# One stage for row norm, turn, product and head norms in five places of a two-block network, and expert prologues tile by tile

## The chip, the cores and the metric

The kernel runs on one core of a Trainium2 chip. The metric is the device time of one execution in microseconds. Five places and two expert layers are edited, so times of places are given from the start of the profiled span.

## The reference, cut to what matters

Two blocks are computed one after the other on 512 tokens of width 1024, all in float32. The first block has two layers, which also carry or read 256 context tokens; each is a mixer followed by an expert layer (16 experts, each with its own choice of tokens):

```
h = rms_norm(x, norm1_g[i]) * (1 + sc1) + sh1        # even: u = h @ ev_w_in; odd: u = h @ od_w_in
q, k = rms_norm(q, q_g), rms_norm(k, k_g)            # odd: 8 heads of 64, in the neighbourhood attention
x = x + g1 * y
h = rms_norm(x, norm2_g[i]) * (1 + sc2) + sh2
aff = softmax(h @ router); gate, idx = top_k(aff per expert); x = x + g2 * experts(h[idx])
```

The second block is a forgetting attention, a gated convolution FFN, a sparse attention on shared keys and values, and a second FFN:

```
proj = rms_norm(x, a_norm) @ a_w_in                  # 3 x 1024 columns for q, k, v and 16 forget columns
q, k = rms_norm(q, q_gain), rms_norm(k, k_gain)      # 16 heads of 64
log_f = log_sigmoid(proj[..., 3072:] + b_f); c = cumsum(log_f)
parts = rms_norm(x, kv_norm) @ kv_w                  # six parts of 2 x 64; ks, kw normed and rotated
proj = rms_norm(x, b_norm) @ b_w_in                  # 1024 columns for q (normed, rotated), 48 for gates
```

## The kernel before

Everything is a sequence of stages (class Stage, line 29): each is a block with one instruction list per engine, which end together before the next begins. Rows of x lie as tiles of 128 tokens (P = 128): LT = 4 tiles of x, CT = 2 of the context, NT = 6 in all. Each product is made of three matmuls, since float32 operands are split in a high part (written by ACT as fp32r) and a low part (the difference, written by DVE): hi x hi, hi x lo, lo x hi.

`norm_turn` (298) is a stage of its own: ACT squares all tiles (337), takes one root for all (340), DVE norms them (363), PE turns them with 512 columns a unit (406), ACT writes the high part with the gain (348, 350), DVE the low part (377); where there is a shift, POOL adds it to the low part (394). `linear` (412) is the next stage: SP asks for weight pieces of 256 columns (452), ACT makes their high part (505), DVE the low part (523), PE multiplies per tile ("tok": rows stationary, 256 weight columns moving) or per 128 weight columns ("feat": weights stationary, tokens moving) in line 493, and DVE keeps each result (540). It has RING = 3 weight slots and eight PSUM buffers. `linear_split` (548) is the like with pieces of 512 columns and half the rows of the weight (588, 602, 612). `head_norm` (634) is a third stage: squares on ACT (681), sums, root and multiply on DVE (697 to 705), the gain on POOL (671), then, with rope, the rotation on DVE (718 to 727).

The five places, in the order of time: (1) even_layer, 1543 and 1552, six tiles, with a shift; (2) odd_layer, 2362 to 2371, six tiles with a shift, whose Q, K and V each have 512 columns, with two stores beside the weights on POOL's queue (461), and two head norms; (3) forgetting, 2545 to 2564, four tiles, with two head norms after `forget_sums` (2458) and a small stage of constants; (4) sparse_attention, 2996 to 3014, the shared keys and values, with three head norms, of which the third is for the compressed keys (they need `compress`, 3010); (5) sparse_attention, 3021 to 3026, with one head norm with rope. In place 3 the forget gate F is a "tok" job of 16 columns, which `forget_sums` then turns on PE (2478).

`mixture` (1130) is one stage of an expert layer. SP loads the norm's gain and two (or one) rows of modulation, broadcast to all partitions (1224 to 1227), then router and four weight quarters. DVE combines the gains (1450) after ACT has squared all tiles (1382) and taken one root (1384), norms tile after tile (1460, 1462), PE turns each (1277), and after the last one PE multiplies all tiles with the router (1284). The softmax, the choice of tokens (1475 to 1477), the gathering by POOL and the stream of 192 weight quarters follow. `add_gated` (1624) is the output product in front of it, by `linear`.

The order on each engine is written out by hand in these functions, and semaphores alone join the engines.

## Time and profile before

| | us |
|---|---|
| median of 3 runs | 5204.43 (5191.65 to 5210.83) |
| the profiled execution, its own time | 5182.43 |
| its span in the trace | 5180.6 |
| PE busy | 4192.4 |
| DVE busy | 3071.3 |
| mean granted clock of PE | 0.879 of full speed |

The span is the time from the first to the last instruction in the trace; around it lie some 1.8 us. Busy is the time in which an engine had an instruction under way. A granted clock of 1 is 2.4 GHz, of 0.5 it is 1.2 GHz. The kernel runs on one core, so no other core shares its time.

### The profile page before, as it was taken

The page shows a single profiled execution, that of the slowest core. Times are in us where ns is not written, and L with a number is a line of the kernel's source. Part 1 is how long each engine was busy: PE and PEld are TensorE (multiplying, and loading weights), DVE is VectorE, ACT ScalarE, POOL GpSimd, SP SyncE. Part 2 cuts the span into 40 slices and gives each one's busy share as a digit, 9 for nine tenths or more (in the row PEclk, how much of TensorE's full clock was granted, in tenths as well). Part 3 has the DMA queues.
Part 4 walks back from the last instruction along what each step waited for, and adds up shares of the span by engine and source line. Part 5 has one row for each costly group of instructions (what it writes and reads, how often), then busy time and mean ns, then how long its engine had stood idle before and what let it go on. Part 6 is the DMA issues. An engine that isn't in the chain of part 4 may idle for free. (4 is left out here: it accounts for less than half of the span.)

```text
span 5180.6 us, 68690 instructions
## 1 busy us (share of the span) xinstructions
PE 4192.4 (81%) x28028; PEld 3310.1 (64%) x28028; DVE 3071.3 (59%) x4349; ACT 1888.9 (36%) x2461; POOL 549.9 (11%) x419
## 2 busy tenths in 40 slices
PE   6868867999956887979669999686799856785998
PEld 2755665666656866869545555465687655674777
DVE  5259946888824556665458888436476234454672
ACT  4122324666622313222126666315322112352221
POOL 0111000111112003323001112002000001000000
PEclk9988787999978997978779999888899967897999
DMA  6120036999930220000249999400122201000322
GB/s 235 54 83 25 1 108 226 364 363 362 334 117 29 74 84 6 3 6 2 100 161 356 365 362 357 159 25 1 56 95 94 92 29 34 1 1 33 114 94 77
DMA packets 246407, 658.34 MB, mean 127 GB/s; under 512 B 27028, under 2 KB 91796, under 8 KB 245576
## 3 DMA queue, kind: packets, MB, share of 16 engines
q1 hardware_dynamic: 227808, 615.14, 33.3%
q0 software_dynamic: 8064, 30.46, 2.2%
q10 hardware_dynamic: 10224, 8.36, 0.5%
q8 instruction: 224, 3.67, 0.3%
q14 instruction: 87, 0.71, 0.0%
HBM read 624.97 MB, written 28.41 MB: 126 GB/s over the span
## 5 line engine op out<-in xcount | busy, mean ns | idle before, releaser
L1426 DVE TENSOR_TENSOR w_lo<-w_quarter,w_hi 128x2048 fp32r<-128x2048 f32 x384 | 874.0, 2287 | 200.0 <-ACT w_hi L1364 198.7
L1364 ACT ACTIVATE w_hi<-w_quarter 128x2048 fp32r<-128x2048 f32 x384 | 735.4, 1917 | 379.2 <-DMA w_quarter<-in_moe_w 188.3
L2682 DVE TENSOR_TENSOR w_lo<-w_chunks,w_hi 128x1024 fp32r<-128x1024 f32 x132 | 161.8, 1226 | 301.4 <-ACT w_hi L2660 301.4
L2634 PE MATMUL ffn_ps<-ffn_inT_hi,w_hi 128*128 128x512 f32 x704 | 276.4, 393 | 16.5 <-DVE w_lo L2682 16.5
L2634 PE MATMUL ffn_ps<-ffn_inT_lo,w_hi 128*128 128x512 f32 x704 | 275.9, 392 | 0.0
L2634 PE MATMUL ffn_ps<-ffn_inT_hi,w_lo 128*128 128x512 f32 x704 | 275.6, 391 | 0.0
L1265 POOL DMA_INDIRECT summed_dram<-gains_then_rows,row_token x32 | 137.9, 4310 | 1005.6 <-DVE gains_then_rows L1445 1005.6
L1312 PE MATMUL down_ps<-w_hi,hiddenT 128*96 128x512 f32 (+1 forms) x512 | 208.1, 406 | 39.2 <-DVE w_lo L1426 26.6
L900 PE MATMUL probT_ps<-ident,prob 128*128 128x128 f32 x896 | 164.6, 301 | 82.6 <-ACT prob L980 80.4
L967 ACT ACTIVATE probT<-probT_ps 128x256 f32<-128x256 f32 (+4 forms) x272 | 142.2, 523 | 223.5 <-PE probT_ps L900 223.5
L1312 PE MATMUL gate_ps<-w_hi,rowsT 128*96 128x512 f32 (+1 forms) x512 | 206.2, 403 | 12.5 <-DVE w_lo L1426 9.6
L1312 PE MATMUL up_ps<-w_hi,rowsT 128*96 128x512 f32 (+1 forms) x512 | 204.7, 400 | 7.4 <-DVE w_lo L1426 7.4
L2660 ACT ACTIVATE w_hi<-w_chunks 128x1024 fp32r<-128x1024 f32 x132 | 138.5, 1049 | 189.4 <-PE ffn_ps L2647 163.7
L1314 PE MATMUL gate_ps<-w_lo,rowsT 128*96 128x512 f32 (+1 forms) x512 | 204.4, 399 | 0.0
L1314 PE MATMUL down_ps<-w_lo,hiddenT 128*96 128x512 f32 (+1 forms) x512 | 204.2, 399 | 0.0
L1314 PE MATMUL up_ps<-w_lo,rowsT 128*96 128x512 f32 (+1 forms) x512 | 201.8, 394 | 0.0
L980 ACT ACTIVATE prob<-score_ps,negmax 128x256 f32<-128x256 f32 (+4 forms) x272 | 166.1, 611 | 87.2 <-DVE negmax L949 85.2
L588 PE MATMUL lin_ps<-w_hi,haT 128*128 128x512 f32 (+1 forms) x576 | 178.8, 391 | 23.3 <-DVE w_lo L612 23.3
L406 PE MATMUL turn_ps<-ident,normed 128*128 128x128 f32 x286 | 58.1, 377 | 166.1 <-DVE normed L363 153.5
L505 ACT ACTIVATE w_hi<-w_landing 128x2048 fp32r<-128x2048 f32 (+4 forms) x39 | 64.7, 1661 | 343.5 <-PE lin_ps L493 221.8
L900 PEld LDWEIGHTS probT_ps<-ident,prob 128*128 128x128 f32 x896 | 106.4, 150 | 126.2 <-ACT prob L980 118.3
L612 DVE TENSOR_TENSOR w_lo<-w_landing,w_hi 128x2048 fp32r<-128x2048 f32 (+2 forms) x28 | 56.2, 2007 | 184.4 <-ACT w_hi L602 184.4
(648 smaller groups left out, 10173.8 us busy)
## 6 DMA issues: line engine op xcount, KB each, us to landing
w_quarter<-in_moe_w SPq DMA_DIRECT2D x384, 1024.0 KB, 6.5
w_chunks<-in_f_w_up SPq DMA_DIRECT2D x88, 512.0 KB, 3.2
ada_landing<-in_ada_w SPq DMA_DIRECT2D x24, 1024.0 KB, 7.0
ada_ring<-in_ada_w SPq DMA_DIRECT2D x24, 1024.0 KB, 5.2
w_chunks<-in_f_w_down SPq DMA_DIRECT2D x44, 512.0 KB, 3.2
w_landing<-in_od_w_in SPq DMA_DIRECT2D x13, 1024.0 KB, 7.2
w_landing<-in_a_w_in SPq DMA_DIRECT2D x12, 1024.0 KB, 5.1
w_landing<-in_ev_w_in SPq DMA_DIRECT2D x6, 1024.0 KB, 7.4
```

The costliest lines, as they stand in the source:

```text
L588: mm = nc.tensor.matmul(ps[n % 2][i][:, 0:width], h[:, g * HK + k, cols], v[:, c % NP, k, 0:width], start=(g + k + j == 0), stop=(g == 1 a ...
L900: mm = nc.tensor.transpose(tps(a, b), pr[:, i % SB, a:b], ident)
L967: nc.scalar.activation(pT[:, i % SB, 0:n], tps(0, n), ACT.Copy).then_inc(tkept, 1)
L980: nc.scalar.activation(pr[:, i % SB, 0:u[1]], score(i, 0, u[1]), ACT.Exp, bias=mx[:, m:m + 1], scale=scale, accum_out=sm[:, m:m + 1]).then ...
L1265: nc.gpsimd.indirect_dma_start(out=sum_dram, out_offset=bass.IndirectOffsetOnAxis(ap=idx[:, e:e + 1], axis=0), in_=ys[e % 2], in_offset=No ...
L1312: nc.tensor.matmul(out[0:R, cols], v[0][:, k, :], wh[c][:, kk, cols], start=first, stop=False, skip_group_check=True)
L1314: nc.tensor.matmul(out[0:R, cols], v[0][:, k, :], wl[c][:, kk, cols], start=False, stop=False, skip_group_check=True)
L1364: nc.scalar.activation(wh[g % NP][:, :, :], land[g % NL][:, :, :], ACT.Copy).then_inc(hi_ready, 1)
L1426: tt(wl[g % NP][:, :, :], land[g % NL][:, :, :], wh[g % NP][:, :, :].bitcast(F32), ALU.subtract) \
L2634: mm = nc.tensor.matmul(ps[c % 4][:, :], w[:, c % NP, cols], h[:, k, :], start=(k + i == 0), stop=(k == KD - 1 and i == 2))
L2660: nc.scalar.activation(wh[:, c % NP, :], land[:, c % NL, :], ACT.Copy).then_inc(hi_ready, 1)
L2682: nc.vector.tensor_tensor(wl[:, c % NP, :], land[:, c % NL, :], wh[:, c % NP, :].bitcast(F32), ALU.subtract).then_inc(split, 1)
```

## The change

`normed_linear` is new and takes the place of norm_turn, linear (or linear_split) and head_norm in the five places. Weight pieces are asked for from the stage's start. Roots, norms, turns, high and low parts go tile by tile, and PE multiplies a tile with the first piece as soon as it is split; turning uses 128 columns an instruction where 512 were used. The shift is added by DVE together with the gain, no longer by POOL. It has four PSUM buffers for products and four for turns, and pieces of 256 columns. Heads are normed by chunks of four heads (a piece), two and three pieces behind the product: squares and root on ACT, sum, multiply and rope on DVE, gain on POOL. In place 2 K comes first, then Q and V; in place 4 the tok job comes before the feat job; the third head norm of place 4 stays a stage. Places 1 and 4 have RING = 2, the others 3. The forget columns become a feat job: 16 weight columns stationary, 512 tokens moving, so F is already turned in forget_sums.

In both expert layers the broadcast gains are loaded by POOL's queue beside the output product in front (`RowGains`), and DVE combines them there after its second piece; roots are taken tile by tile, and the router's product of a tile follows the turn of the next. The odd layer's output product has three weight slots where it had two.

The diff, cut to its core:

```diff
@@ linear @@
-def linear(nc, h, K, w, jobs, RING=3, whole=None, low_from=None, beside=(), mod=None):
+def linear(nc, h, K, w, jobs, RING=3, whole=None, low_from=None, beside=(), mod=None, then=None):
...
+                if c == 1 and then is not None:
+                    dve.wait_ge(beside_done, 16 * len(beside))
+                    then()
@@ new function @@
+def normed_linear(nc, x, segments, h, w, jobs, ident, heads=(), RING=3, beside=()):
...
+    PW, NB, HK, HD = 256, 4, KD // 2, 64
+    wv = w.rearrange("(k p) n -> p k n", p=P)
+    pieces = [(job, a, min(a + PW, job[2])) for job in jobs for a in range(0, job[2], PW)]
...
+            for c, (job, a, b) in enumerate(pieces):
+                if c >= RING:
+                    sp.wait_ge(split, c - RING + 1)
+                sp.dma_start(land[:, c % RING, :, 0:b - a], wv[:, :, job[1] + a:job[1] + b]).then_inc(landed[c % RING], 16)
+
+        @block.gpsimd
+        def _(pool):
+            if beside:
+                pool.wait_ge(rows_split, 2 * nt)
+            for dst, src in beside:
+                pool.dma_start(dst, src).then_inc(beside_done, 16)
+            for i, c in enumerate(order):
+                z, gain, _, _ = normed_heads[c]
+                pool.wait_ge(head_normed, i + 1)
+                nc.gpsimd.tensor_tensor(z, z, gain.unsqueeze(1).unsqueeze(1).broadcast_to(list(z.shape)), ALU.mult) \
+                    .then_inc(head_gained, 1)
+            if order:
+                pool.wait_ge(head_gained, len(order))
+            if beside:
+                pool.wait_ge(beside_done, 16 * len(beside))
+
+        @block.tensor
+        def _(pe):
+            def turn_tile(i):
+                pe.wait_ge(normed, i + 1)
+                for half in range(2):
+                    if i >= 2:
+                        pe.wait_ge(rows_split if not shifted else moved, 2 * (i - 2) + half + 1)
+                    for k in range(HK):
+                        kk = half * HK + k
+                        mm = nc.tensor.transpose(tp[i % 2 * 2 + half][:, k, :], xn[:, i % 2, kk * P:(kk + 1) * P],
+                                                 ident)
+                    mm.then_inc(turned, 1)
+
+            u = 0
+            turn_tile(0)
+            turn_tile(1)
+            for c, piece in enumerate(pieces):
+                job, a, b = piece
+                pe.wait_ge(split, c + 1)
+                for unit in units(piece):
+                    if u >= NB:
+                        pe.wait_ge(kept, u - NB + 1)
+                    if job[0] == "tok":
+                        t = unit[0]
+                        if c == 0:
+                            pe.wait_ge(rows_split, 2 * tiles.index(t) + 2)
+                        out = ps[u % NB][:, 0:b - a]
+                        cols = slice(t * P, (t + 1) * P)
+                    else:
+                        f, (r0, r1) = unit
+                        m = min(P, b - f * P)
+                        out = ps[u % NB][0:m, 0:r1 - r0]
+                        cols = slice(r0, r1)
+                        fs = slice(f * P - a, f * P - a + m)
+                    for j, (r, v) in enumerate(((hh, wh), (hh, wl), (hl, wh))):
+                        for k in range(KD):
+                            if job[0] == "tok":
+                                lhsT, rhs = r[:, k, cols], v[:, c % RING, k, 0:b - a]
+                            else:
+                                lhsT, rhs = v[:, c % RING, k, fs], r[:, k, cols]
+                            mm = nc.tensor.matmul(out, lhsT, rhs, start=(j + k == 0), stop=(j == 2 and k == KD - 1))
+                    mm.then_inc(summed, 1)
+                    if c == 0 and u + 2 < nt:
+                        turn_tile(u + 2)
+                    u += 1
+
...
+            def rows_hi_part(i):
+                t = tiles[i]
+                gain, shift = column[t]
+                cols = slice(t * P, (t + 1) * P)
+                for half in range(2):
+                    ks = slice(half * HK, (half + 1) * HK)
+                    if shift is not None:
+                        act.wait_ge(moved, 2 * i + half + 1)
+                        nc.scalar.activation(hh[:, ks, cols], part[:, half], ACT.Copy).then_inc(rows_hi, 1)
+                        continue
+                    act.wait_ge(turned, 2 * i + half + 1)
+                    for k in range(HK):
+                        kk = half * HK + k
+                        ins = nc.scalar.activation(hh[:, kk, cols], tp[i % 2 * 2 + half][:, k, :], ACT.Copy,
+                                                   scale=gain[:, kk:kk + 1])
+                    ins.then_inc(rows_hi, 1)
...
+            act.wait_ge(eps_ready, 1)
+            for i in range(3):
+                root(i)
+            for i in range(nt):
+                rows_hi_part(i)
+                if i == 0:
+                    hi_part(0)
+                if i + 3 < nt:
+                    root(i + 3)
+                if i == nt - 2:
+                    hi_part(1)
+            for c in range(2, RING):
+                hi_part(c)
+            for c in range(RING, len(pieces) + RING + 2):
+                hi_part(c)
+                head_square(c - RING)
+                head_roots(c - RING - 1)
...
+            def rows_lo_part(i):
+                t = tiles[i]
+                gain, shift = column[t]
+                cols = slice(t * P, (t + 1) * P)
+                for half in range(2):
+                    ks = slice(half * HK, (half + 1) * HK)
+                    src = tp[i % 2 * 2 + half]
+                    if shift is not None:
+                        dve.wait_ge(turned, 2 * i + half + 1)
+                        if i:
+                            dve.wait_ge(rows_split, 2 * i + half - 1)
+                        for k in range(HK):
+                            kk = half * HK + k
+                            ins = nc.vector.tensor_scalar(part[:, half, k, :], src[:, k, :], gain[:, kk:kk + 1],
+                                                          shift[:, kk:kk + 1], ALU.mult, ALU.add)
+                        ins.then_inc(moved, 1)
+                        if 2 * i + half:
+                            shifted_lo(2 * i + half - 1)
+                        continue
+                    dve.wait_ge(rows_hi, 2 * i + half + 1)
+                    for k in range(HK):
+                        kk = half * HK + k
+                        ins = nc.vector.scalar_tensor_tensor(out=hl[:, kk, cols], in0=src[:, k, :],
+                                                             scalar=gain[:, kk:kk + 1], in1=hh[:, kk, cols].bitcast(F32),
+                                                             op0=ALU.mult, op1=ALU.subtract)
+                    ins.then_inc(rows_split, 1)
...
+            norm(0)
+            norm(1)
+            first_units = units(pieces[0])
+            for i in range(nt):
+                rows_lo_part(i)
+                if i == 0:
+                    lo_part(0)
+                if i + 2 < nt:
+                    norm(i + 2)
+                if i >= NB - 1:
+                    keep_unit(0, i - NB + 1, first_units[i - NB + 1])
+                if i == nt - 2:
+                    lo_part(1)
+            if shifted:
+                shifted_lo(2 * nt - 1)
+            for c in range(2, RING):
+                lo_part(c)
+            u = 0
+            for c, piece in enumerate(pieces):
+                for unit in units(piece):
+                    if c or u >= max(0, nt - NB + 1):
+                        keep_unit(c, u, unit)
+                    u += 1
+                lo_part(c + RING)
+                head_sum(c - 1)
+                head_scale(c - 2)
+                head_rope(c - 3)
+            n = len(pieces)
+            head_sum(n - 1)
+            head_scale(n - 2)
+            head_rope(n - 3)
+            head_scale(n - 1)
+            head_rope(n - 2)
+            head_rope(n - 1)
+            if order:
+                dve.wait_ge(head_gained, len(order))
@@ mixture @@
+        self.loads = [(self.hid[:, :], d["norm2_g"][i].partition_broadcast(P))]
+        for r in range(rows):
+            self.loads.append((self.gain[:, r, :], mod_dram[r, 4 * D:5 * D].partition_broadcast(P)))
+            self.loads.append((self.shift[:, r, :], mod_dram[r, 3 * D:4 * D].partition_broadcast(P)))
+
+    def combine(self):
+        for r in range(self.rows):
+            self.nc.vector.scalar_tensor_tensor(out=self.gain[:, r, :], in0=self.gain[:, r, :], scalar=1.0,
+                                                in1=self.hid[:, :], op0=ALU.add, op1=ALU.mult)
...
-            sp.dma_start(ng[:, :], d["norm2_g"][i].partition_broadcast(P)).then_inc(consts, 16)
-            for r in range(NROW):
-                sp.dma_start(gain[:, r, :], mod_dram[r, 4 * D:5 * D].partition_broadcast(P)).then_inc(consts, 16)
-                sp.dma_start(shift[:, r, :], mod_dram[r, 3 * D:4 * D].partition_broadcast(P)).then_inc(consts, 16)
...
+            def logits(t):
+                if t == 0:
+                    pe.wait_ge(router_landed, 16)
+                pe.wait_ge(n_kept, 2 * t + 2)
+                for k in range(KD):
+                    mm = nc.tensor.matmul(pl[:, t, :], nT[:, k, t * P:(t + 1) * P], rw[:, k, :],
+                                          start=(k == 0), stop=(k == KD - 1), skip_group_check=True)
+                return mm
+
             for t in range(nt):
                 pe.wait_ge(h_ready, t + 1)
                 if t >= 2:
@@ -1277,13 +1631,9 @@
                     mm = nc.tensor.transpose(bank[t % 2][:, k * P:(k + 1) * P], h[:, t, k * P:(k + 1) * P], ident)
                     if k % HK == HK - 1:
                         mm.then_inc(n_turned, 1)
-            pe.wait_ge(router_landed, 16)
-            for t in range(nt):
-                pe.wait_ge(n_kept, 2 * t + 2)
-                for k in range(KD):
-                    mm = nc.tensor.matmul(pl[:, t, :], nT[:, k, t * P:(t + 1) * P], rw[:, k, :],
-                                          start=(k == 0), stop=(k == KD - 1), skip_group_check=True)
-            mm.then_inc(scored, 1)
+                if t:
+                    logits(t - 1)
+            logits(nt - 1).then_inc(scored, 1)
...
+            def root(t):
                 if t:
                     act.wait_ge(squared, t)
                 nc.scalar.activation(junk[:, :], x[:, t, :], ACT.Square, accum_out=ss[:, t:t + 1]).then_inc(squared, 1)
-            act.wait_ge(mean_ready, 1)
-            nc.scalar.activation(rs[:, :], ss[:, :], ACT.Sqrt).then_inc(root_ready, 1)
+                act.wait_ge(squared, t + 1)
+                nc.scalar.activation(rs[:, t:t + 1], ss[:, t:t + 1], ACT.Sqrt, bias=eps[:, :], scale=1.0 / D) \
+                    .then_inc(root_ready, 1)
+
+            act.wait_ge(eps_ready, 1)
+            for t in range(min(3, nt)):
+                root(t)
...
+                if t + 3 < nt:
+                    root(t + 3)
@@ add_gated @@
-        linear(nc, (hh, hl), K, w, [("tok", 0, D, tiles, keep)], RING=3 if n == TOK else 2, whole=inT)
+        linear(nc, (hh, hl), K, w, [("tok", 0, D, tiles, keep)], whole=inT, beside=beside, then=then)
@@ odd_layer @@
+                heads = [(c + i, (buf[:, :, :].rearrange("p t (h d) -> p t h d", h=H8)[:, 0:n, 4 * i:4 * i + 4, :],
+                                  cst[gain], scale, None))
+                         for c, buf, n, gain, scale in ((0, K, NT, "na_k_g", 1.0), (2, Q, LT, "na_q_g", 0.125))
+                         for i in range(2)]
+                normed_linear(nc, x, [(0, LT, gm[:, 0, :], modT[:, 0, :, 0]), (LT, CT, gm[:, 1, :], modT[:, 0, :, 1])],
+                              (hh, hl), d["od_w_in"],
+                              [("tok", RWI + 512, 512, tiles, keep(K)), ("tok", RWI, 512, tiles[:LT], keep(Q)),
+                               ("tok", RWI + 1024, 512, tiles, keep(VN))], ident, heads,
+                              beside=[(low_dram, hl[:, :, :]), (x_kept, x[:, 0:LT, :])])
@@ forget_sums @@
-            pe.wait_ge(ready, 1)
-            for t in range(LT):
-                mm = nc.tensor.transpose(ps[0:H16, t * P:(t + 1) * P], F[:, t, :], ident)
-            mm.then_inc(turned, 1)
+            chain(nc.vector.tensor_scalar(F, F, b_f, None, ALU.add))
@@ forgetting @@
+        normed_linear(nc, x, [(0, LT, cst["a_norm"], None)], (hh, hl), d["a_w_in"],
+                      [("tok", i * D, D, tiles, keep(buf)) for i, buf in enumerate((Q, K, V))] +
+                      [("feat", 3 * D, H16, [(0, SEQ)], keep_forget)], ident, heads)
+        forget_sums(nc, F[:, :], cst["a_b_f"], negs[:, :])
@@ sparse_attention @@
-            linear(nc, (hT, hTl), KD, d["kv_w"], [("feat", 0, 256, [(0, SEQ)], keep_raw), ("tok", 256, 512, tiles, keep_two)], RING=2)
+            normed_linear(nc, x, [(0, LT, cst["kv_norm_2"], None)], (hT, hTl), d["kv_w"],
+                          [("tok", 256, 512, tiles, keep_two), ("feat", 0, 256, [(0, SEQ)], keep_raw)], ident, heads, RING=2)
+            head_norm(nc, zc[:, :, :, :], [0], 2, 64, cst["kc_gain"], rope=([0], 0, 1, 8, C[:, LT:], Sn[:, LT:]))
+        normed_linear(nc, x, [(0, LT, cst["b_norm"], None)], (hh, hl), d["b_w_in"],
+                      [("tok", 0, D, tiles, keep(Q)), ("tok", D, 48, tiles, keep(gt))], ident, heads)
```

## Rows read from the trace of the kernel before

**Rows 1.** The page, busy time, share of the span and instructions of each engine
```profile
PE 4192.4 (81%) x28028; PEld 3310.1 (64%) x28028; DVE 3071.3 (59%) x4349; ACT 1888.9 (36%) x2461; POOL 549.9 (11%) x419
```

**Rows 2.** Busy time by stretch: PE, PEld, DVE, ACT, POOL, clock, DMA share, GB/s
```profile
108.00:272.00 164.00, 129.17 (x864) 118.33 (x864) 45.25 (x67) 31.44 (x37) 19.58 (x16) 0.88 0.14 43
1450.00:1621.00 171.00, 105.15 (x816) 102.16 (x816) 60.97 (x87) 36.06 (x48) 36.55 (x28) 0.80 0.20 68
3293.00:3525.00 232.00, 158.25 (x708) 133.10 (x708) 86.75 (x89) 48.15 (x47) 24.68 (x9) 0.79 0.17 55
4143.00:4270.00 127.00, 71.50 (x416) 67.77 (x416) 44.35 (x126) 22.78 (x38) 4.08 (x9) 0.66 0.10 31
4277.00:4390.00 113.00, 66.25 (x320) 57.86 (x320) 47.87 (x60) 22.50 (x28) 12.15 (x4) 0.75 0.12 39
747.00:795.00 48.00, 27.91 (x144) 26.14 (x144) 17.39 (x17) 16.73 (x27) 0.00 (x0) 0.61 0.77 283
2618.00:2654.00 36.00, 20.17 (x96) 19.19 (x96) 12.62 (x14) 10.71 (x18) 0.00 (x0) 0.59 0.77 287
```

**Rows 3.** Timeline, start of place 3: start us, duration us, engine, line, instruction, count, [idle before]
```profile
3293.01 1.06 ACT L337 ACTIVATE squares<-x 128x1024 f32<-128x1024 f32 x1 [20.96 <-PEq L67]
...
3297.72 1.28 ACT L340 ACT_TABLE_LOAD   x1
...
3299.46 2.74 DVE L363 TENSOR_SCALAR normed<-x,inverse_root 128x1024 f32<-128x1024 f32 x4
...
3315.75 1.91 ACT L602 ACTIVATE w_hi<-w_landing 128x2048 fp32r<-128x2048 f32 x1 [6.51 <-DMA w_landing<-in_a_w_in]
3317.70 2.29 DVE L612 TENSOR_TENSOR w_lo<-w_landing,w_hi 128x2048 fp32r<-128x2048 f32 x1 [7.36 <-ACT w_hi L602]
...
3320.04 0.79 PE L588 MATMUL lin_ps<-w_hi,haT 128*128 128x512 f32 x1 [11.82 <-DVE w_lo L612]
```

**Rows 4.** Timeline of PE, first matmuls of place 1's product
```profile
152.84 2.07 PE L493 MATMUL lin_ps<-w_hi,h1T 128*128 128x256 f32 x8 [16.04 <-DVE w_lo L523]
...
156.40 1.10 PE L493 MATMUL lin_ps<-w_hi,h1T_low 128*128 128x256 f32 x8
```

**Rows 5.** Groups by form, 1450 to 1622: count, busy us, mean ns, idle before
```profile
L377 DVE SCALAR_TENSOR_TENSOR low_unshifted<-turn_ps,gm,h1T_hi 128x512 f32<-128x512 f32 x8 | 6.0, 750 | 2.7 <-POOL h1T_low_1a L394 1.4 <-PE turn_ps L406 0.8
...
L377 DVE SCALAR_TENSOR_TENSOR low_unshifted<-turn_ps,gm,h1T_hi 128x256 f32<-128x256 f32 x8 | 3.9, 484 | 5.6 <-POOL h1T_low_1a L394 5.6
```

**Rows 6.** Timeline of DVE, place 1, last keep of the first weight piece
```profile
171.67 0.43 DVE L1547 COPY mla_in<-lin_ps 128x256 f32<-128x256 f32 x1 [2.40 <-PE lin_ps L493]
```

**Rows 7.** Timeline of DVE, last keeps of places 3, 4 and 5
```profile
3454.00 0.69 DVE L2548 COPY fa_v<-lin_ps 128x512 f32<-128x512 f32 x1 [2.06 <-PE lin_ps L588]
...
3471.34 0.17 DVE L2548 COPY fa_f<-lin_ps 128x16 f32<-128x16 f32 x1 [2.39 <-PE lin_ps L588]
...
4206.32 0.28 DVE L3004 COPY v_win<-lin_ps 128x128 f32<-128x128 f32 x1
...
4363.89 0.21 DVE L2973 COPY branch_gates<-lin_ps 128x48 f32<-128x48 f32 x1 [2.35 <-PE lin_ps L588]
```

**Rows 8.** Timeline around head norms of places 2, 3; then two lines' durations, ns min/median/max
```profile
1593.39 2.19 ACT L681 ACTIVATE squares<-x 128x512 f32<-128x512 f32 x4 [50.65 <-PEq L67]
...
3482.80 3.90 ACT L681 ACTIVATE squares<-fa_q 128x1024 f32<-128x1024 f32 x4 [4.56 <-PEq L67]
...
3524.53 0.61 POOL L809 COPY twice<-fa_q 128x512 f32<-128x512 f32 x1 [0.60 <-POOL fa_k L671]
...
L705 DVE TENSOR_TENSOR fa_q<-fa_q,root x4: 1218/2290/3360, 3489.8 to 3495.4; 128x1024 f32<-128x1024 f32 x4
...
L671 POOL TENSOR_TENSOR fa_q<-fa_q,a_q_gain x4: 2334/3281/3317, 3491.2 to 3500.9; 128x1024 f32<-128x1024 f32 x4
```

**Rows 9.** Timeline of the first expert layer's start
```profile
757.82 2.36 DVE L1450 SCALAR_TENSOR_TENSOR gains_then_rows<-gains_then_rows,hidden 128x1024 f32<-128x1024 f32 x2 [11.10 <-DMA gains_then_rows<-mod_rows]
...
777.51 17.39 PE L1284 MATMUL misc_ps<-router,normedT 128*128 128x16 f32 x96
```

276 lines of the change are left out of this document (195 added, 81 removed).

## The prediction

> **What bounds the kernel now.** I read the page's busy line first: PE is busy for 81% of the span and no other engine above 60% [rows 1]. So the reader should not look for a busier engine but for stretches in which PE stands. The windows view shows seven of them around the edited code: in five places and in front of both expert layers the granted clock averages 0.59 to 0.88 and PE is busy for 56 to 79% of the stretch [rows 2]. The timeline of one place shows why: the stages follow each other. In the forgetting layer the squares start at 3293.0, the table for the root is loaded, four tiles are normed and turned, only then does the next stage ask for its weights, and the first matmul of the product comes at 3320.0 [rows 3]. Place 1 repeats this with 44 us (squares with the start of its stretch in [rows 2], first matmul at 152.8 [rows 4]), the other three with 46, 27 and 26. After the products PE stands again while the heads are normed: 1593.4 to 1621 in place 2, 3482 to 3524.5 in place 3 and 4363.9 to 4390 in place 5 [rows 2, 7, 8].
>
> **Start of the five places.** I walk one tile through the new stage. Squares 1.06 plus 0.19 for the sum, table 1.28, root 0.2, norm 0.75 [rows 3]: the first normed tile stands 4 us after the start. Turning, hi and lo of it take some 5 us. The first weight piece was asked for at the start and split by ACT (1.9) and DVE (2.3) behind that: first matmul after 12.6 us in an unshifted place. In a shifted place (1 and 2) the second half's lo of tile 0 stands behind the next tile's parts on DVE, some 15.5 us. A tile then costs what the slowest engine needs. Today's instruction on 512 columns takes 0.750 and on 256 0.484 [rows 5]; the slope gives 0.35 for 128, or 0.28 from start to start since records overlap by some 0.07. Eight of them are 2.25 us. Shifted, DVE does parts 2.25, two subtractions 1.4, norm 1.0, keep 0.42: 5.1 us. Unshifted, ACT and DVE each have 3.4 to 4, and PE, with 24 matmuls (2.83, a keep and the idle time before it in [rows 6]) and eight transposes (1.1), 3.95. So the first piece ends, with six shifted tiles: DVE is through with the first weight split at 12.4, then five tiles' parts and subtractions 18.3, four norms 4.0, three keeps 1.3, the second split 2.3, one last subtraction 0.7, and PE's last unit 2.83 with its waits, **42.3** us after the start. With four unshifted: 12.6, a first unit at the low clock 4.5, tiles two and three at the pace of ACT and DVE with the second split in their way 9.7, the last unit 2.83, **29.6**.
>
> The bounds for the small instruction are 0.18 (half of 0.35) and 0.48 (the 256-column row); I take 0.28, and the ends move a tile by about 1 us, 24 us in all. On this the Trainium skill (VectorE: DVE Perf Modes, "The TRN2 errata") speaks against the change: it says that many small tiles pay a fixed latency each and wants 512 elements or more. From its PSUM row for 128 elements I would estimate 0.26 us, with which the sum would be the same within 4 us; by its rule and by the slope of the rows alike, cutting 512 columns in four adds 1.3 us of work a tile.
>
> Place 1: today the first piece ends at 171.7 [rows 6], 63.2 after the squares; new 42.3: **21**. Place 2: from the squares to the head norms 143 today [rows 2, 8]. New: 42.3, then 26 units of 24 matmuls at 2.83 = 73.6, and a tail of 5.3 for the last Q chunk (scale 1.22, gain on POOL 2.3 to 3.3 [rows 8], small ones): 21.5 saved, plus today's head norms, 27.9 [rows 2, 8]: **49**.
>
> Place 3 (forgetting): today 3293.0 to the last keep at 3471.3, 178.3 [rows 3, 7]. New: 29.6, then 11 pieces x 11.33 = 124.6, then the forget columns. Today these 96 matmuls of 16 columns take from 3454.0 to 3471.3, 17.3 us [rows 7]: 0.18 each, for 128 weight columns are loaded for 16 that move, and the clock falls meanwhile. New: 24 matmuls with 512 moving columns, 5.5 us at 2.75 per dozen. Sum 160: 18 saved, the turn of F saves 1, and the two head norms, from 3482.8 (after the constants) to 3524.5 [rows 8], 41.7, go entirely, since eight Q and K chunks are done beside V: **61**. Pieces of 256 instead of 512 columns cost 2.83 a unit against 2.75 per half tile; the 11.33 contains that.
>
> Place 4: today 62.6 from the squares at 4143.8 to the last keep [rows 7]; new 29.6 + 11.3 + 11 (two features at 512) + tail 5.6: 5 saved. Two of the three small head norms leave, 11.6 net of the table load that the third then pays: **17**. Place 5: today 86.6 to 4363.9 [rows 7]; new 28.3 (the table is already there) + 3 x 11.33 + 10.2 for the gates, unchanged: 14. Then today's head chain of 26.1 shrinks to the last chunk's sum and the last two's scale, gain and turn: 11.5, with 6.5 (a quarter) and 26 as bounds: 14.5. **28**.
>
> **Expert prologues.** Today the gains land 11 us into the stage and PE scores the tiles only after all are turned, 17.4 us for six [rows 9]. New: gains are ready, tile 0 is normed 5.6 us after the start, and PE takes a turn (27.9 busy less 17.4 for the scores, over six: 1.8) and a score (17.4/6 = 2.9) per tile, 4.7, more than DVE's two passes. With a first turn and its waits the scores end at 782 instead of 794.9 [rows 2, 9]: 12.5, and by four tiles 9.5 in the second layer. Top-k, gather and the weight stream follow unchanged, so this passes on. The five (three) gain loads move from SP's queue there to POOL's in the output product before; they run beside its first weight, which I let land 2 (1.5) us later, bounds 0 and 5. The combine, 2.4 and 1.2 us of DVE, is covered by eight PSUM buffers; without them it is a price of 2.4. **10.5 and 8.**
>
> **What waits behind what.** DVE's queue holds, between the keeps of two pieces: wait for the hi part 1.9, lo 2.3, head sum 1.4, scale 1.6, with rope some 1.5 more. That is 7 to 9 us and with keeps below 11.33, the time in which PE fills four buffers. [Rows 8] show what a gain on POOL adds: the same multiply of DVE takes 1.22 alone and 3.36 when it starts inside one. I count one such hold of 2.1 a piece, in the slack. POOL issues the two stores of place 2 before its first gain; nobody waits for these before the end.
>
> **Sum.** 21 + 49 + 61 + 17 + 28 + 10.5 + 8 = 194.5. I take 12 off: in the first pieces PE has holes after every tile, and the row of expert layer 0 [rows 2] shows 0.61 granted at PE 58% busy, against 1.0 in unbroken products, so part of them will run at 1.2 GHz. 182 off the profiled execution's 5182.4 is 5000; that execution lies 22 below the median of 5204.4, from which I get 5022. Small: the third ring slot in the odd output product (0 to 1), RING=2 in place 1 (the next split has 17 us for 4.2), F's bias (0.2).
>
> **Rivals.** *The clock stays at 1.2 GHz through the first pieces.* A tile then costs PE 7.6 us instead of 5.1 or 4: 12 x 2.5 + 12 x 3.6 = 73, of which 22 are in my walk and the 12. That leaves 131 saved, 5073. For: all seven stretches show less than 0.9. Against: at the low clock PE would be the slowest and unbroken, and after 152.8 eight matmuls of 256 columns took 2.07 us and the third such group 1.10 [rows 4]. The Trainium skill (TensorE: Matmul & The Clock Gate, "A second HAM failure mode: psum-queue depth-cycling") holds that short idles between groups alone make the clock swing; by it this rival holds in each of the five places.
> *The change doesn't shorten the ends:* head norms and scores move but DVE or the weights end the stage as late. Then only the starts count, about 21 + 24 + 18 + 5 + 14 = 82: 5122. Against: DVE is busy for 28 to 42% of these stretches [rows 2].
> *Slower:* DVE's turn between two pieces isn't covered. It decides once that turn, 7 to 9 us by my count, exceeds the 11.33 of four units and PE stands for all of it and more: 29 later pieces at 8 us are 232 against 182 saved, 50 slower: 5254. Against: lo parts are three pieces ahead, and today's PE doesn't stop at the 2.29 us of one.
>
> **Numbers.** Forecast 0.74, clock rival 0.17, ends not shortened 0.05, slower 0.02, and 0.02 for no change. 0.5%, 26 us, is about what a measurement can tell: faster 0.95, same 0.02, slower 0.03. The range runs from 219 saved (small instructions at the low bound and no clock loss) to 5085, which takes in the clock rival and the tails' upper bounds.
>
> **Right or wrong by.** First product matmul 12 to 16 us after the squares; first pieces ending at 42 and 30; no head norm between product and stack turn in places 2 and 3; one group of 24 matmuls of 512 columns at the end of place 3; scores done 35 and 26 us after the prologue's start. Wrong if PE shows gaps of several us at each w_lo, if a multiply on DVE is held 3 us per chunk in front of a lo part, or if transposes and first units run at double time throughout.

## The result and the profile after

The changed kernel takes **5023.9 us** (median of 4 runs, 5013 to 5034) against 5206.3 (4 runs, 5192 to 5211) on the same chip: ratio **0.9662, 95% interval [0.9637, 0.9687]**. A second series on another chip gave 5020.5 against 5185.7, ratio 0.9674 [0.9646, 0.9702]. The forecast was 5022.

The page's busy line and the seven stretches of [rows 1, 2], by the windows view of the changed kernel (columns as in [rows 2]):

```profile
PE 4183.2 (83%) x28720; PEld 3337.1 (66%) x28720; DVE 3099.8 (62%) x4544; ACT 1895.9 (38%) x2548; POOL 484.4 (10%) x383
...
107.00:260.00 153.00, 130.41 (x864) 120.10 (x864) 59.32 (x116) 29.89 (x39) 0.00 (x0) 0.91 0.16 46
1442.00:1572.00 130.00, 102.58 (x816) 101.08 (x816) 68.14 (x131) 33.67 (x45) 13.38 (x7) 0.91 0.26 90
3230.00:3401.00 171.00, 150.10 (x1208) 146.12 (x1208) 86.86 (x151) 51.19 (x78) 19.14 (x8) 0.94 0.25 75
4019.00:4137.00 118.00, 76.00 (x434) 72.27 (x434) 47.65 (x123) 28.20 (x63) 5.83 (x9) 0.67 0.11 34
4137.00:4231.00 94.00, 70.59 (x512) 69.86 (x512) 52.21 (x104) 26.29 (x57) 9.46 (x5) 0.78 0.16 48
739.00:777.00 38.00, 30.63 (x144) 30.12 (x144) 16.45 (x21) 18.19 (x34) 0.00 (x0) 0.54 0.76 288
2562.00:2589.00 27.00, 20.60 (x96) 20.09 (x96) 11.89 (x17) 11.67 (x23) 0.00 (x0) 0.55 0.86 324
```

PE does nearly the same work in shorter stretches: it is busy for 85% of place 1, 79% of place 2 and 88% of place 3, where [rows 2] have 79, 61 and 68%.

Most of the rest is read from one table: the length of each stretch in the profiles, from the start of one instruction to that of another (in place 1 to the end of the keep). There are two profiles of each kernel; "all" is the mean of the ten profiles (experiments among them) that have the new expert layer's code. What is saved is the difference of the two means, for the expert layers that to "all".

```
stretch                                      before          after          forecast saved   saved
place 1: squares to last gate keep           163.3, 163.8    151.6, 150.5        21          12.5
place 2: squares to first stack copy (ACT)   172.9, 172.4    130.6, 131.4        49          41.7
place 3: squares to first stack copy (POOL)  231.5, 232.0    170.8, 169.6        61          61.6
place 4: squares to place 5's squares        133.5, 133.6    117.7, 117.7        17          15.8
place 5: squares to first stack copy (POOL)  113.4, 116.3     93.6,  93.6        28          21.2
expert layer 0: squares to place 2's         703.1, 700.4    703.9, 697.8       10.5          2 (all 699.5, 689 to 708)
expert layer 1: squares to place 3's         674.9, 670.9    667.7, 668.3         8           4.5 (all 668.4, 661 to 675)
```

That is 159 us. The spans of the two profiles of each kernel differ by 162 (5180.6 and 5182.7 against 5021.2 and 5018.6). The working promised 182 between profiled executions, so it was **about 20 us too generous**. The medians differ by 182 and 165 in the two series, and 5022 was met because the forecast added to 5000 the 22 us by which the first profile lies below its median, while the profiled execution of the changed kernel, 5023.0, lies within 1 us of its median. The two errors cancel: that the median hit 5022 is luck.

**Places 1 and 2, first piece.** A unit is the 24 matmuls of one tile with one piece. PE's timeline in place 2 (start, duration, engine, line, instruction, count, idle before and what ended it), squares at 1442.8, and then DVE's:

```profile
1446.61 3.68 PE L636 MATMUL turn_ps<-ident,normed 128*128 128x128 f32 x16 [23.25 <-DVE normed L753]
1458.14 2.05 PE L667 MATMUL lin_ps<-w_hi,h1T_hi 128*128 128x256 f32 x8 [7.85 <-DVE h1T_low_1a L766]
...
1465.43 1.21 PE L667 MATMUL lin_ps<-w_hi,h1T_hi 128*128 128x256 f32 x8 [1.62 <-DVE h1T_low_1a L766]
...
1471.03 1.21 PE L667 MATMUL lin_ps<-w_hi,h1T_hi 128*128 128x256 f32 x8 [1.62 <-DVE h1T_low_1a L766]
...
1484.88 1.25 PE L667 MATMUL lin_ps<-w_hi,h1T_hi 128*128 128x256 f32 x8 [4.26 <-DVE h1T_low_1a L766]
```

```profile
1463.41 1.37 DVE L781 TENSOR_SCALAR shifted<-turn_ps,gm,modT 128x128 f32<-128x128 f32 x4 [2.48 <-PE turn_ps L636]
1464.69 0.68 DVE L766 TENSOR_TENSOR h1T_low_1a<-shifted,h1T_hi 128x512 fp32r<-128x512 f32 x1
...
1469.01 1.37 DVE L781 TENSOR_SCALAR shifted<-turn_ps,gm,modT 128x128 f32<-128x128 f32 x4 [0.70 <-PE turn_ps L636]
```

The first matmul comes 15.3 us after the squares, as forecast (15.5). The second unit starts 7.3 us later, behind a first one at half the clock; from there the units come every 5.60 us, and while PE waits 1.62 for DVE's lo, DVE waits 2.48 and 0.70 for PE's turn: neither is the slowest engine, they wait for each other. Then comes one wait of 4.26 behind the second weight split, and the piece ends 49.4 us after the squares, not 42.3.

**Place 3** (squares at 3230.3), its first product, the forget columns, their keep and the first stack copy:

```profile
3241.99 2.07 PE L667 MATMUL lin_ps<-w_hi,haT 128*128 128x256 f32 x8 [4.59 <-DVE w_lo L760]
...
3384.55 2.02 PE L667 MATMUL lin_ps<-haT,w_hi 128*16 128x512 f32 x8
...
3390.31 0.68 DVE L2893 COPY fa_f<-lin_ps 16x512 f32<-16x512 f32 x1 [5.14 <-PE lin_ps L667]
...
3401.03 0.61 POOL L1138 COPY twice<-fa_q 128x512 f32<-128x512 f32 x1 [34.47 <-SPq L67]
```

First matmul after 11.7 us, last keep after 160.0 (160 was forecast), the forget columns in 5.8 us for the 17.3 of [rows 7], and no head norm before the stacks.

**Place 5**, keeps and head work of DVE around the gate columns, and the windows view of these columns:

```profile
4199.29 0.42 DVE L3318 COPY nb_q<-lin_ps 128x256 f32<-128x256 f32 x1 [2.46 <-PE lin_ps L667]
...
4206.21 0.32 DVE L3318 COPY branch_gates<-lin_ps 128x48 f32<-128x48 f32 x2
4211.05 0.21 DVE L3318 COPY branch_gates<-lin_ps 128x48 f32<-128x48 f32 x1 [4.52 <-PE lin_ps L667]
4216.17 0.21 DVE L3318 COPY branch_gates<-lin_ps 128x48 f32<-128x48 f32 x1 [4.91 <-PE lin_ps L667]
4216.29 1.21 DVE L810 TENSOR_REDUCE head_sums<-head_squares 128x16 f32<-128x1024 f32 x1
...
4229.08 0.42 DVE L836 TENSOR_TENSOR nb_q<-nb_q,rope_part 128x256 f32<-128x256 f32 x1
```

```profile
4199.90:4216.20 16.30, 16.23 (x90) 16.11 (x89) 6.66 (x13) 1.16 (x2) 2.36 (x1) 0.59 0.00 0
```

The last Q column is kept 62.3 us after the squares at 4137.4, as the working has it (28.3 and three pieces of 11.33). Then the gate columns keep PE busy for another 16.3 us at a granted clock of 0.59, never idle, and 13.2 us of head work follow alone. All four gate units, the matmuls beside that last Q keep included, take 17.0 us (4199.1 to 4216.1).

**Expert layer 0.** The gather of the first rows, the weight loads issued behind it and the turn of the rows, first in the changed kernel, then in the kernel before:

```profile
803.12 2.90 POOL L1593 DMA_INDIRECT gains_then_rows<-normed_dram,row_token  x1 [144.08 <-DVE row_token L1835]
805.20 4.77 SPq L1569 DMA_DIRECT2D w_quarter<-in_moe_w  x3
...
811.60 0.72 PE L1650 MATMUL misc_ps<-ident,gains_then_rows 96*128 96x96 f32 x3 [9.05 <-DMA gains_then_rows<-normed_dram,row_token]
```

```profile
822.26 1.03 POOL L1249 DMA_INDIRECT gains_then_rows<-normed_dram,row_token  x1 [402.30 <-DVE row_token L1484]
...
824.61 4.77 SPq L1221 DMA_DIRECT2D w_quarter<-in_moe_w  x3
...
826.45 1.51 PE L1300 MATMUL misc_ps<-ident,gains_then_rows 96*128 96x96 f32 x8 [4.77 <-DMA gains_then_rows<-normed_dram,row_token]
```

Scores end 36.9 us after the squares instead of 47.8: 10.9 gained. But before, the gather's instruction was over (823.3) when the next three megabytes of weights were issued (824.6), and now it is not (806.0 against 805.2). Its rows are turned 8.5 us after it began instead of 4.2, and 4.3 of the 10.9 are gone. In expert layer 1 nothing of this kind changed, for there the first gather was the long one already in the kernel before:

```profile
2674.61 2.90 POOL L1249 DMA_INDIRECT gains_then_rows<-normed_dram,row_token  x1 [202.50 <-DVE row_token L1484]
```

Its rows were turned 9.2 us after it began there and 8.3 in the changed kernel, the scores end after 25.6 us instead of 35.5, and the first gate matmul comes after 57.0 instead of 67.7.

### The profile page after: what moved, and what is told of

It reads as the page before. It is cut to its first block and busy times, and to the rows that moved or that the text cites. A ratio compares the mean times of both kernels' runs of the same rounds, so it can differ in the third digit from the quotient of the medians.

```text
span 5021.2 us, 70146 instructions
## 1 busy us (share of the span) xinstructions
PE 4183.2 (83%) x28720; PEld 3337.1 (66%) x28720; DVE 3099.8 (62%) x4544; ACT 1895.9 (38%) x2548; POOL 484.4 (10%) x383
## 5 line engine op out<-in xcount | busy, mean ns | idle before, releaser
L1662 PE MATMUL down_ps<-w_hi,hiddenT 128*96 128x512 f32 (+1 forms) x512 | 208.0, 406 | 43.3 <-DVE w_lo L1783 30.4
L1229 PE MATMUL probT_ps<-ident,prob 128*128 128x128 f32 x896 | 166.3, 304 | 87.7 <-ACT prob L1309 85.4
L1609 POOL DMA_INDIRECT summed_dram<-gains_then_rows,row_token x32 | 122.6, 3832 | 1034.9 <-DVE gains_then_rows L1802 1034.9
L1662 PE MATMUL gate_ps<-w_hi,rowsT 128*96 128x512 f32 (+1 forms) x512 | 205.9, 402 | 12.2 <-DVE w_lo L1783 9.6
L1662 PE MATMUL up_ps<-w_hi,rowsT 128*96 128x512 f32 (+1 forms) x512 | 204.8, 400 | 11.8 <-DVE w_lo L1783 11.7
L2979 PEld LDWEIGHTS ffn_ps<-ffn_inT_hi,w_hi 128*128 128x128 f32 x704 | 133.2, 189 | 45.0 <-DVE w_lo L3027 17.3
L1668 PE MATMUL gate_ps<-w_hi,rowsT 128*96 128x512 f32 (+1 forms) x512 | 162.7, 399 | 0.0
L1668 PE MATMUL down_ps<-w_hi,hiddenT 128*96 128x512 f32 (+1 forms) x512 | 162.6, 399 | 0.0
L1668 PE MATMUL up_ps<-w_hi,rowsT 128*96 128x512 f32 (+1 forms) x512 | 160.2, 394 | 0.0
```

Of the source, the lines that this page charges most:

```text
L1229: mm = nc.tensor.transpose(tps(a, b), pr[:, i % SB, a:b], ident)
L1609: nc.gpsimd.indirect_dma_start(out=sum_dram, out_offset=bass.IndirectOffsetOnAxis(ap=idx[:, e:e + 1], axis=0), in_=ys[e % 2], in_offset=No ...
L1662: nc.tensor.matmul(out[0:R, cols], v[0][:, k, :], wh[c][:, kk, cols], start=first, stop=False, skip_group_check=True)
L1668: mm = nc.tensor.matmul(out[0:R, cols], v[1][:, k, :], wh[c][:, kk, cols], start=False, stop=last, skip_group_check=True)
L2979: mm = nc.tensor.matmul(ps[c % 4][:, :], w[:, c % NP, cols], h[:, k, :], start=(k + i == 0), stop=(k == KD - 1 and i == 2))
```

## The experiments

All start from the changed kernel; the diffs are in the new stage unless another function is named. "Place" times are the stretches of the table.

**1. Both lo halves of a shifted tile at once** (DVE's queue in places 1 and 2).

```diff
-                            dve.wait_ge(rows_split, 2 * i + half - 1)
+                            dve.wait_ge(rows_split, 2 * i)
...
                         ins.then_inc(moved, 1)
-                        if 2 * i + half:
-                            shifted_lo(2 * i + half - 1)
                         continue
...
                 rows_lo_part(i)
+                if shifted:
+                    shifted_lo(2 * i)
+                    shifted_lo(2 * i + 1)
```

> In places 1 and 2 DVE now takes both lo halves of a tile right behind its eight shifted parts, instead of the second half's behind the next tile's first four parts. Theory A (why the first pieces of places 1 and 2 end about 8 us later than forecast): the second lo waits for the next tile's turn, and PE does that turn only behind the product of the tile before, so PE and DVE wait for each other and a tile takes 5.6 us. Then the first product matmul comes 12.5 us after the squares instead of 15.4, a tile takes 5.1 to 5.3 us, the first piece ends some 43 to 45 us after the squares instead of 50, and each of the two places is 5 to 7 us shorter, 5012 in all. Rival B: DVE is simply the busiest engine and its small instructions are dearer than I took them: the order changes nothing but the first matmul, tiles stay at 5.6 us, the total within 3 us of 5024. Places 3 to 5 hold no shift and stay as they are in both.

Measured: 5020.8 us, ratio to the kernel before 0.9687 [0.9657, 0.9716]: the medians can't tell it from the changed kernel. The stretches can. Place 1 fell to 146.6 and place 2 to 125.9, 4.5 and 5.1 us below the means of the changed kernel. PE in place 2, squares at 1433.9:

```profile
1446.44 2.08 PE L667 MATMUL lin_ps<-w_hi,h1T_hi 128*128 128x256 f32 x8 [5.28 <-DVE w_lo L760]
...
1452.21 1.19 PE L667 MATMUL lin_ps<-w_hi,h1T_hi 128*128 128x256 f32 x8
...
1456.15 1.21 PE L667 MATMUL lin_ps<-w_hi,h1T_hi 128*128 128x256 f32 x8
...
1460.95 1.22 PE L667 MATMUL lin_ps<-w_hi,h1T_hi 128*128 128x256 f32 x8 [0.82 <-DVE h1T_low_1a L766]
...
1473.52 2.04 PE L667 MATMUL lin_ps<-w_hi,h1T_hi 128*128 128x256 f32 x8 [4.27 <-DVE h1T_low_1a L766]
```

First matmul after 12.5 us, the second unit 5.8 later, three more every 3.9 to 5.2, the last 7.3 behind the fifth, and the first piece at an end after 44.7. Theory A holds; B, dearer small instructions, falls: DVE's instructions are the same, only their order isn't. The tiles in the middle became even a little shorter than A had them.

**2. All turns ahead of the product.**

```diff
-            turn_tile(0)
-            turn_tile(1)
+            for i in range(nt):
+                turn_tile(i)
...
-                    if c == 0 and u + 2 < nt:
-                        turn_tile(u + 2)
```

> PE turns all tiles before the first product matmul; everything else of the new stage stays (first weights asked for at once, heads inside). Theory A (the starts gain because the first piece's products run between the turns of later tiles): the first product matmul comes only when the last tile is turned, about 22 us after the squares with four tiles and 33 us with six, and the first piece then needs its four or six units of 2.85 us behind that, so the first pieces end at about 34 instead of 30 and 52 instead of 50 us: 4 us in each of places 3, 4 and 5 and 2 us in places 1 and 2, 16 in all, 5040. Rival B (the gain of the starts lies in the overlap of product and turn, not in the early weights and the joined stages): the starts fall back by most of what they saved, 80 us, 5105. Rival C: unbroken products afterwards run at the full clock at once and the order is as good as the new one, 5024.

Measured: 5033.0 us, 0.9695 [0.9666, 0.9723]. Places 1 to 5: 152.4, 132.2, 171.6, 119.0, 95.6, which is 1.3, 1.2, 1.4, 1.3 and 2.0 more, 7 us in all. The first matmuls came at 29.4, 17.1 and 15.9 us, earlier than A had it for four tiles. So B falls, and even A gave this overlap twice its worth: when all tiles stand ready, the units of places 3 to 5 follow each other every 2.9 us from the second on, which makes up for most of the late start. C would have had no loss; the 7 us are small, but all five places show them.

**3. Heads as stages of their own.** No `heads` in places 2 to 5; `head_norm` follows as before.

```diff
-                              [...], ident, heads, ...)
+                              [...], ident, ...)
+            for buf, ts, gain, scale in (...):
+                head_norm(nc, buf[...], ts, ..., cst[gain], scale=scale)
```

> The new stage without heads in places 2 to 5; the head norms follow as stages of their own as in the kernel before. Theory A (head work inside the stage is hidden beside the products, as forecast): it adds in place 2 27.9 less the tail of 5, in place 3 41.7, in place 4 11.6, in place 5 26.1 less a tail of 13 that the trace shows: 23 + 42 + 12 + 13 = 90, so 5114. Rival B (the DVE work of the heads delays keeps and weight splits inside the stage, so part of it is paid there): the product stages get shorter by some us each when the heads leave, and less than 75 is lost, under 5100.

Measured: 5114.9 us, 0.9859 [0.9826, 0.9893]. Places 2 to 5: 154.8, 210.9, 124.1, 106.2: 23.8, 40.7, 6.4 and 12.6 more, 84 us. In place 3 PE stands again from product to stacks:

```profile
3420.00:3462.00 42.00, 0.07 (x1) 0.00 (x0) 29.89 (x33) 13.41 (x15) 14.43 (x5) 0.56 0.00 0
```

A holds, but for place 4, where it had 11.6. The product stages are no shorter without the heads: DVE's head work costs the product nothing.

**4 and 11. The old expert prologue**, twice: `mixture` of the kernel before, no gains loaded in the output product.

```diff
-        gains = RowGains(nc, ctx, d, 0, 2, mod_dram)
-        add_gated(..., gains.loads, gains.combine)
+        add_gated(..., (), None)
```

> The two expert layers have the prologue of the kernel before again (gains loaded inside the layer, mean and root for all tiles at once, scores behind all turns). Theory A (what the scores gain passes on to the end, the forecast): 11 in the first layer and 10 in the second come back, 5045. Rival B (the first layer's gain was given back because its weight stream runs at what the DMA queues deliver and doesn't end earlier): only the second layer's 8 come back, 5032, and the first layer takes 686 us from squares to the last row store with either prologue. To be read in both profiles: time from the first squares to the end of each expert layer, and the length of the weight stream, 608 us before and 620 after in the first layer, 603 and 605 in the second; if these lengths scatter by 10 us from profile to profile where nothing in the layer differs, the loss in the first layer is scatter and not the change's doing.

> The kernel with the old expert prologues a second time, for its profile alone. With the new prologue eight profiles gave 694 to 708 us from the first layer's squares to place 2's, mean 701, and 662 to 675 for the second, mean 669; with the old one two profiles gave 703 and 716, and 675 and 671. Theory A (the prologue's gain of about 10 us a layer is passed on, under a scatter of as much): 705 to 716 and 672 to 680. Rival B (the stream decides and nothing is passed on): about 701 and 669. The first gate matmul comes 83 to 90 us after the squares instead of 75.5 in the first layer and 63 to 68 instead of 57 in the second, in both.

Measured: 5040.1 us, 0.973 [0.9704, 0.9755], and one run of 5039.7. Expert layer 0 took 715.8 and 715.0 us, layer 1 671.1 and 674.5; with the new prologue the means are 699.5 and 668.4. So inside this kernel the prologues are worth 16 and 4.4 us; the first is clear of the scatter (689 to 708), the second lies within it (661 to 675). B of the first of these expectations, nothing in layer 0, falls; A had 11 and 10. The first gate matmul comes after 89.4 us in layer 0 in both, for 75.6 on average with the new prologue, and after 63.2 and 62.3 in layer 1, for 57.3: what a prologue gains up to there is passed on in layer 0, and the time behind it, 626 and 610 us, is about as long as with the new prologue (624 and 611). The 16 are more than the kernels differ in layer 0 (table), in part because the old prologue does worse here than it did in the kernel before: its scores take 20.5 us at a granted clock of 0.50 throughout where they took 17.4 at 0.60 (16.4 in experiment 12), and its gather is slow as well (2.91). That makes 7.6 us up to the first gate matmul; another 6 come behind it (626 for 620), and nothing shows why. These are the scores' rows in the windows view, here and in the kernel before:

```profile
766.10:786.60 20.50, 20.50 (x98) 20.41 (x96) 0.00 (x0) 1.89 (x3) 0.00 (x0) 0.50 0.49 180
```

```profile
777.50:794.90 17.40, 17.40 (x98) 17.29 (x96) 0.00 (x0) 1.88 (x3) 0.00 (x0) 0.60 0.59 213
```

**5. The changed kernel again.**

> The changed kernel once more, unaltered, so that the others of this series are held against it on the same chip, and to see how far one profiled execution of it lies from the next. Theory A (the stretches that no edit touches scatter): the stretch from the first expert layer's squares to place 2's squares takes 697 to 708 us and the second layer's 667 to 675 (so far 704, 703, 699 and 708, and 668, 672, 675 and 668, with the same code), while each of the five places repeats within 1 us. Rival B (each kernel has its own fixed times): both repeat the 704 and 668 of the first profile within 1 us.

Measured: 5020.5 us, 0.9674 [0.9646, 0.9702]. The places repeat within 1.2 us, a little more than the 1 expected, layer 0 took 697.8, layer 1 668.3. A holds, with layer 0 at the lower edge of its range. The largest scatter is in code that no edit touches: from place 2's stacks to layer 1's squares ten profiles gave 972 to 1001 us, which is what blurs the medians.

**6. Forget columns as moving data again**, with the old `forget_sums`.

```diff
-                      [("feat", 3 * D, H16, [(0, SEQ)], keep_forget)], ident, heads)
-        forget_sums(nc, F[:, :], cst["a_b_f"], negs[:, :])
+                      [("tok", 3 * D, H16, tiles, keep(F))], ident, heads)
+        forget_sums(nc, F[:, :, :], cst["a_b_f"], negs[:, :], ident)
```

> In the forgetting layer the 16 forget columns are a token-wise job again (token tiles as weights, 16 columns moving), turned afterwards in the sums' stage as before; the rest of the new stage stays. Theory A: 96 matmuls of 16 columns cost 16 to 17 us instead of 5.7, and the turn and its waits 1 to 2: the stretch from place 3's squares to the stacks grows from 170 to 182 to 184. Rival B: as the head work beside V is now done by then and PE is the only one left, nothing hides them and they cost more than before, because the clock falls earlier in the run of small matmuls: 187 or more. Rival C: DVE's last head work was what ended the stage, and the stage grows by less than 8.

Measured: 5031.1 us, 0.9708 [0.9677, 0.9739]; place 3 took 181.1, 10.9 more than the mean of 170.2. The columns took from 3371.4 to 3388.0, 16.6 us, and matmuls of one form became slower in them although PE never stood:

```profile
3373.15 1.93 PE L667 MATMUL lin_ps<-w_hi,haT 128*128 128x16 f32 x16
...
3381.05 3.56 PE L667 MATMUL lin_ps<-w_hi,haT 128*128 128x16 f32 x16
```

Sixteen of them take 1.93 us at first and 3.56 later. A holds, 1 us short; B and C fall.

**7. Lo halves, early weight part, early tail**: experiment 1 and

```diff
-                if i == nt - 2:
+                if i == 1:
                     hi_part(1)
...
             for c, piece in enumerate(pieces):
+                if early and c == n - 1:
+                    ends(n - 1)
                 for unit in units(piece):
```

where `early` says that the last piece is token-wise and has no head, and `ends` is the head work that stood behind the loop.

> Three edits at once, each in its own place of the trace. (1) Both lo halves of a shifted tile at once, as in the first of these experiments (place 1 fell from 151.6 to 146.6). (2) ACT makes the hi part of the second weight piece behind tile 1 instead of behind the last tile but one: if DVE's wait for it is what makes PE stand 4.3 us in front of the last units of the first piece, places 1 and 2 lose another 2 us (144.5 in place 1) and places 3 to 5 up to 1 us; if that weight split itself (2.3 us of DVE) is the cost, nothing changes. (3) In place 5 DVE does the last two chunks' head work ahead of the four keeps of the gate columns, for which the four PSUM buffers wait: Theory A, DVE stands idle for 9.4 us between these keeps and then works 13 us alone, so the stretch from place 5's squares to the stacks falls from 93.6 to 84 to 85. Rival B, the head of this chunk is held by ACT's square and root and the gain on POOL, and no more than 3 us are saved. All together 5024 less 10 to 12, 3 and 9: 5000, or 5012 if only the lo halves count.

Measured: **4997.7 us, 0.9637 [0.9608, 0.9667]**. Place 1: 144.9, place 2: 122.7 (another 1.7 and 3.2 from the early part); places 3 and 4 unchanged; place 5: 83.4, 10.2 less. PE's last wait of the first piece in place 2, and DVE in place 5:

```profile
1462.82 1.19 PE L667 MATMUL lin_ps<-w_hi,h1T_hi 128*128 128x256 f32 x8 [3.40 <-DVE h1T_low_1a L766]
```

```profile
4206.94 0.42 DVE L834 TENSOR_TENSOR nb_q<-nb_q,rope_part 128x256 f32<-128x256 f32 x1
4207.40 0.55 DVE L3327 COPY branch_gates<-lin_ps 128x48 f32<-128x48 f32 x4
```

The wait is 3.40 instead of the 4.27 of experiment 1: DVE's wait for ACT was only its smaller part, and most of the rest is the split of 2.29 us in DVE's queue. The gate keeps now come at the end, together, and nothing waits for them. With squares at 1424.2 the first piece of place 2 ends at 1465.7, 41.5 us later; the 42.3 of the forecast is what DVE's queue allows in this order, and not in the one that the change has.

**8. PE kept busy ahead of the first product.**

```diff
             turn_tile(1)
+            for i in range(16):
+                nc.tensor.transpose(ps[NB - 1][:, i % 4 * P:(i % 4 + 1) * P], ident, ident)
```

> Between the first two turns and the first product PE does 16 idle turns of the identity into the PSUM buffer that is used last, so that it is not idle there. Theory A (the first unit of 24 matmuls takes 5 us instead of 2.85 because the clock is at its lower level after PE's wait): the granted clock is up when the product starts, the first unit takes about 3 us and each of the four-tile places ends 1.5 to 2 us earlier: places 3 and 4 from 160.0 and 117.7 to 158.3 and 116. In places 1 and 2 DVE holds the tiles anyhow and less than 1 us is gained. In all 5 to 8 us, 5018. Rival B (the level is set by more than the engine's being busy just before): the first unit stays at 5 us and all is as before. Rival C: the clock then falls again in the gaps behind later units and the gain is given back.

Measured: 5014.4 us, 0.9684 [0.9647, 0.9722], which by itself tells nothing. Places 3, 4 and 5: 167.0, 116.1 and 92.3, which is 3.2, 1.6 and 1.3 less; places 1 and 2 as they were. The windows of the two real turns, the idle turns and the first unit of place 3, and the same first unit in the changed kernel (granted clock is the eighth number):

```profile
3215.40:3218.90 3.50, 3.48 (x17) 3.48 (x18) 1.65 (x5) 3.44 (x13) 0.00 (x0) 0.50 1.10 350
3218.90:3221.00 2.10, 2.07 (x17) 1.83 (x16) 1.43 (x6) 2.10 (x4) 0.00 (x0) 0.92 1.09 347
3223.30:3226.30 3.00, 2.95 (x25) 2.95 (x26) 2.96 (x11) 1.09 (x5) 0.00 (x0) 1.00 0.57 158
```

```profile
3242.00:3247.20 5.20, 5.20 (x24) 5.20 (x25) 3.65 (x12) 1.03 (x4) 0.00 (x0) 0.50 0.64 202
```

A holds: 3.0 instead of 5.2 us for the first unit at 2.4 instead of 1.2 GHz, and the clock doesn't fall again in the next units.

**9. The edits of 7 and 8 together.**

> The three edits of the run before together with the sixteen idle turns in front of the first product. In their own stretches the single edits gave: lo halves, early hi part and tail 6, 8 and 10 us in places 1, 2 and 5; the idle turns 1.3 to 2.6 us in each of places 3, 4 and 5 and nothing sure in 1 and 2. Theory A (they touch different waits and add up): place 1 145, place 2 121 to 123, place 3 167, place 4 116, place 5 82, which is 29 to 31 us less than the changed kernel, a median near 4992 where that has 5020. Rival B (in place 5 the first unit's 2 us are not passed on, since DVE's head work now ends the stage): place 5 stays at 83 to 84. Rival C: in places 1 and 2, with DVE's order mended, PE is the slower one in the first units, so that the idle turns now gain 1 to 2 us there as well: place 1 at 143.

Measured: **4979.7 us, 0.9608 [0.9582, 0.9635]**, the fastest, and clear of the changed kernel's interval. Places: 145.7, 124.1, 166.3, 116.8, 81.5. Against the means of the changed kernel that is 29 us less, as A has it, though place 2 stayed above its 121 to 123; place 5 fell below 83 (B falls) and places 1 and 2 gained nothing from the idle turns (C falls). The median lies 12 us under A's 4992, which the places don't explain; layer 0 was the shortest of all profiles here, 689.

**10. The old order inside the new stage**: experiment 2, and the first weights asked for when all tiles are turned and split only then.

```diff
         def _(sp):
+            sp.wait_ge(turned, 2 * nt)
             for c, (job, a, b) in enumerate(pieces):
```

(`hi_part(0)`, `hi_part(1)`, `lo_part(0)` and `lo_part(1)` stand behind the loops over the tiles, and so do all keeps.)

> Inside the new stage the old order: all tiles are turned, then the first weights are asked for, then split, then the product; heads stay inside. With all turns first but the weights early the first matmul came at 29.4, 17.1, 17.1 and 15.9 us after the squares and the places were only 1 to 2 us longer. Theory A (what the starts gained is above all the weights' latency and their split, not product beside turn): the first matmul comes 8 to 11 us later still, at 38 to 40 in places 1 and 2 and 26 to 28 in places 3 to 5, and each place is 9 to 12 us longer than with the weights early: place 1 162 to 165, place 3 181 to 184, place 4 129 to 131, place 5 105 to 107; 50 to 60 us in all, a median near 5080. Rival B (the saving came from the small steps of norm and turn, tile by tile, and the weights were never late): no more than 4 us a place on top, under 5055.

Measured: 5063.2 us, 0.9775 [0.9743, 0.9807]. First matmuls at 35.9 (places 1, 2), 24.7, 24.5 and 23.3; places 156.5, 136.0, 179.0, 127.0, 103.0. Against experiment 2 that is 4.1, 3.8, 7.4, 8.0 and 7.4 more, 31 us: less than A, more than B's 4 in three places. The late request costs 6.5 to 7.6 us at the first matmul. In place 3 it was issued at 3231.9, 15.1 us after the squares.

**12. The kernel before again.**

> The kernel before once more, for a second profile of it: the one that the forecast was made from lies 22 us below the median of its runs, and in it the first expert layer took 703 us from its squares to place 2's squares where two profiles with the same prologue in the changed kernel gave 716 and 715. Theory A (that profile was a lucky one in this layer: its gathered rows came 4 us sooner and its scores ran 3 us shorter): 712 to 718 here, the first gate matmul 86 to 90 us after the squares instead of 82.9, and the five places repeat within 1 us (163.3, 172.9, 231.5, 133.5, 113.4). Rival B (something of the kernel before makes this layer shorter than in the changed one, so the new prologue brings nothing): 703 again.

Measured: 5184.9 us. Layer 0 took 700.4, its first gate matmul came after 80.7, and the first gather took 1.03 us again. B holds as far as the layer's length goes: the kernel before does have the shorter gather and the quicker scores each time. Of the places only 5 was off, 116.3 for 113.4.

## Why the forecast came out as it did

- **First matmul, forget job, scores: right.** 15.3 and 11.7 us for 15.5 and 12.6; 5.8 for 5.5; scores ending at 36.9 and 25.6 us for 35 and 26.
- **"A tile then costs what the slowest engine needs": the step that failed in places 1 and 2** (21 and 49 forecast, 12.5 and 41.7 saved). DVE's 5.1 us a tile was sized well enough; its eight parts take 2.6 for the 2.25 of the working. What was missed is the order in its queue. The second lo of a tile stood behind the first parts of the next tile; these need that tile's turn, and PE makes it only after the product of the tile before. So every tile went once through PE's queue and back. Experiment 1 opened that loop, experiment 7 took the rest. I had seen the order, but charged it once, at the first matmul, and not for every tile.
- **Place 3: right in sum and in parts.** 61.6 for 61; heads 40.7 (experiment 3, forecast 41.7), forget columns 10.9 (experiment 6, forecast 12.8 with the turn), start 8.8 (experiment 10 against the mean of 170.2; the working had 18 less the columns' 11.8).
- **Place 5: the term for the gates was mis-sized.** "10.2 for the gates, unchanged" is four times the 2.56 us from one gate keep to the next (0.21 and the 2.35 before it in [rows 7]). But in the kernel before only twelve matmuls lie between two such keeps, the second half of each sum; the first halves of all four, 48 matmuls, ran ahead of them from 4348.8 to 4354.2. All 96 took 15.1 us there. Now 16.3 follow the last Q keep (the window above). That is 6 of the 8 us by which the first pair of profiles (113.4 to 93.6) falls short of 28; the tail, 13.2 for 11.5, is the rest. The working let the one follow the other, as they do here; in experiment 7 DVE's head work runs beside the gate columns, and the place is 10.2 us shorter. The term for place 4's head norms, 11.6, was 6.4 by experiment 3, made up by its start (9.3 by experiment 10).
- **Expert prologues: the scores gained what was forecast, 10.9 and 9.9 us; "so this passes on" failed at layer 0's gather.** 4.3 of the 10.9 were lost there. That the rows got in line with the weights is argued from the order of the issues, and not shown: in all profiles of either layer a gather instruction of 2.9 us, the loads issued 2.1 us after its start and late rows go together, and no run moved the loads. From the first gate matmul to the next stretch layer 0 took 620 us before and 624 on average after (614 to 632), layer 1 605 and 611 (604 to 617). With this scatter and two profiles of the kernel before, these last 4 and 6 us can't be put down to anything; experiments 4 and 11 show no such loss from the prologue. The 2 us charged for the first weight beside the gain loads did not show: its hi part starts 5.4 us after the load's issue, for 5.5 before.
- **The 12 us for the clock** were mostly spent on other things. The first unit of a place takes 4.6 to 5.2 us, most of it at 1.2 GHz, where 2.85 is the full rate. The walk already had 4.5 for it in places 3 to 5, and with that unit at the full rate (experiment 8) these three places gained 6.1 us, places 1 and 2 nothing. The fifth unit of places 1 and 2 is slow as well, behind the idle 4.25 and 4.26, by some 2 us each. The rest of the 12 stood in for the terms above: 194.5 were added up and 159 came. The holes of 1.62 us after every tile cost no clock: from 1463.0 to 1485.0, with three of them and the 4.26 inside, 1.00 was granted:

```profile
1463.00:1485.00 22.00, 12.87 (x105) 11.95 (x104) 18.44 (x43) 7.57 (x11) 0.00 (x0) 1.00 0.04 6
```

So the clock rival falls. The Trainium skill (TensorE: Matmul & The Clock Gate, "A second HAM failure mode: psum-queue depth-cycling"), which would have the clock swing at such holes, isn't borne out in these places.
- **Ends not shortened, slower:** both rivals fall by experiment 3: with the heads as stages of their own the places are 84 us longer and the products no shorter; in the profile of the changed kernel PE has no hole at the later w_lo of any place.
- **The starts** were put at 82 us, the forget columns among them, and give 69. (The 24 in that sum for place 2 is a slip; its own working has 21.5.) They are 7 for product beside turns (experiment 2), 31 for the early weights (experiment 10 against 2), 11 for the forget columns, and 20 that stay in places 1 and 2 when the old order is restored inside the new stage (156.5 for 163.6; 136.0 for 172.7 less the heads' 23.8). There the first matmul comes at 35.9 us where the old stages had 44.3 and 46.5. That these 20 come from norming and shifting tile by tile is argued, not shown; no run put the shift back on POOL.
- **Small instructions: taken rightly at 0.28, but "1.3 us of work a tile" for cutting is too much.** In an unshifted place eight of them, here in place 5, start every 0.26 us:

```profile
4154.30 2.16 DVE L790 SCALAR_TENSOR_TENSOR hqT<-turn_ps,b_norm,hqT 128x128 fp32r<-128x128 f32 x8 [2.76 <-ACT hqT L706]
```

The 0.26 that the prediction gave beside its own 0.28 is what the trace shows there; the shifted kind starts every 0.32. The 1.3 counted records in full (eight of 0.35 against two of 0.75). From start to start the instructions on 512 columns took 0.66 in the kernel before where nothing held them (3307.6 to 3308.9), so cutting costs some 0.8 us a tile.

## What to carry to other kernels

When two engines serve each other in turns, don't cost a step by the busier of them: write out each one's queue and follow one item through it; here moving one subtraction a tile forward in DVE's queue gave 5 us a place, and keeps for which nobody waits gave 10 when they were put behind work that was waited for. Joining stages pays most through what it lets start early (first weights) and through the work of a second engine that disappears beside the first (heads), and least through product beside preparation. And count a prologue's gain where the work behind it starts: of 10.9 us at the scores 4.3 were gone at the gather, and with two profiles of a stretch that scatters over 18 us, a gain of a few us can't be read from its length at all.

## What the runs showed of the hardware

- An unbroken PE can lose its clock: in place 5's matmuls of 48 moving columns it was granted 0.59 over 16.3 us with 16.23 busy, and in experiment 6 sixteen matmuls of 16 moving columns went from 1.93 to 3.56 us.
- The clock can rise during turns: it went from 0.50 to 0.92 during an unbroken run of 32 of them (experiment 8), sixteen taking 3.68 us and the next sixteen 2.08. The Trainium skill (TensorE: Matmul & The Clock Gate, "Part 4: PE-mode transpose") says that the full rate doesn't engage for transposes; these turns, in f32, show otherwise.
- The first gather of expert layer 0 took 1.03 us on POOL in both profiles of the kernel before and 2.90 or 2.91 in all twelve others, with the old prologue too; that of expert layer 1 took 2.88 to 2.91 in all fourteen. Rows were turned 4.2 or 4.3 us after the start of a short one and 8.3 to 9.6 after that of a long one. Why it is long wasn't found.
